# A decoder step on one core: the memory merge multiplied as rounded parts, and a third pair of split buffers from the output projection on

## The chip, the cores and the metric

The kernel runs on one core of one Trainium2 chip. The metric is device time in microseconds (us) of one execution, the median of several. The engines are TensorE (PE in the profile), VectorE (DVE), ScalarE (ACT), GpSimd (POOL) and SyncE (SP), which here only issues loads and stores.

## The reference, cut to what matters

One step of a hybrid decoder over 512 prompt tokens and 8 x 4 sample tokens (T = 544 columns in all), in float32. Three branches (latent attention, a state-space scan, attention into a memory) are projected, gated and summed; then come the output projection, a layer norm, a feed-forward part in two halves, and a second layer norm.

```python
def _merge_ffn(x, o_mla, o_ssm, o_mem, g_raw, b_gate, w_o_mla, w_o_ssm, w_o_mem, w_out,
               ln1_g, ln1_b, w_up, b_up, w_down, b_down, ln2_g, ln2_b):
    g = jax.nn.sigmoid((g_raw + b_gate).astype(F32)).astype(x.dtype)
    g_a, g_b, g_m = jnp.split(g, N_BRANCH, axis=-1)
    m = g_a * (o_mla @ w_o_mla) + g_b * (o_ssm @ w_o_ssm) + g_m * (o_mem @ w_o_mem)
    x1 = _layer_norm(ALPHA * x + m @ w_out, ln1_g, ln1_b)
    h = jnp.square(jax.nn.relu(x1 @ w_up + b_up))
    return _layer_norm(ALPHA * x1 + h @ w_down + b_down, ln2_g, ln2_b)
```

The change concerns the term `g_m * (o_mem @ w_o_mem)` with its gate projection (the memory merge), the product with `w_out` and the first layer norm.

## The kernel before

Activations lie with features on the 128 partitions and the 544 tokens in the free dimension, 8 chunks of 128 features for a width of 1024. Weights come as one stream of 128 x 1024 blocks (512 KB), loaded by SP into a ring of four slots; a block gives one output chunk of 128 features from 8 input chunks. There are two accumulators in PSUM, acc[0] and acc[1], each with two halves of 272 tokens.

A block is multiplied in one of two ways.
- As float32 (`project`, L1650 to L1665): 16 matmuls, which the profile shows as 32 instructions.
- As rounded parts (`project_parts`, L1706 to L1727, with `products`, L1700): weight and activation are each the sum of a rounded part and a remainder, both of type fp32r, and a product becomes three matmuls (rounded x rounded, rounded x remainder, remainder x rounded), 48 for a block. The activations' parts are made once; each weight block is split on its way: ACT copies it from the ring into a rounded buffer (L674), POOL subtracts that from the block into the remainder buffer (L498).

All order is written out by hand, with semaphores. `hi_ready` passes a block from ACT to POOL, `split_ready` from POOL to PE, and PE increments `split_begun` with the first matmul of a block. There are two pairs of split buffers, so that ACT may fill the pair of block i once block i-1 has begun (and block i-2 is therefore over).

The stages that the text speaks of, in order:
- Memory attention: PE reads cached values in (`cached_mem_values`), interleaved with the first merge. Its last piece increments `mem_used` to 16.
- Memory merge (phase merge_m, L2172 to L2181): for each of 8 output chunks j a float32 block with the gate weights on X (accumulator 0) and a float32 block with w_o_mem on the branch output BR (accumulator 1). ACT turns accumulator 0 into the gate (`read_gate`, L876). DVE multiplies it with accumulator 1 (L1584), adds it to the sum MG (L1588), rounds it (L1590, MG_H) and takes the remainder (L1592, MG_L, then `mg_ready`). Between the first two blocks PE turns the sample part of the memory attention, which DVE copies into BR (L1577).
- Output projection (out): 8 split blocks on MG_H, MG_L; `sums` on DVE adds accumulators to X and collects means and squares.
- First layer norm: `normalize` on DVE (L1050 to L1100), roots, gain and rounding on ACT (L653 to L663), half of the centring and of the remainders on POOL (L508, L512). Its normed chunks come one after the other, and `project_pair` multiplies each with the first two up blocks at once, so that both pairs of split buffers are in use until its end.
- Up and down projections in two halves (up0, down0, up1, down1), all as rounded parts; then the second layer norm and the stores.

## Time and profile before

| | us |
|---|---|
| median of 3 runs | 1771.91 |
| lowest, highest | 1770.88, 1776.06 |
| the profiled execution, its own time | 1772.24 |
| its span, first to last instruction | 1770.6 |
| TensorE busy in it | 1697.0 (96%) |
| mean granted TensorE clock | 0.984 of full |

The profile is of one execution. Its times count from the first instruction. A busy time is the union of an engine's instructions, a mean is of one instruction; matmuls overlap, so the distance from start to start says what one costs. "PE" rows are matmuls, "PEld" rows weight loads that run beside them. In square brackets at the end of a timeline row stands the idle time before it and what ended it.

### The profile page before, as it was taken

Reading aid. Unit: us, or ns where it says so; the run is one execution under the profiler, and the core shown is the slowest. Engines: PE = TensorE matmul, PEld = TensorE weight load, DVE = VectorE, ACT = ScalarE, POOL = GpSimd, SP = SyncE. Lnnn points to the kernel's source line nnn. Section 1 sums busy time; section 2 is a strip of 40 time slices with the busy share of each in tenths; the row PEclk is TensorE's granted clock in tenths of the full one; section 3 lists DMA queues with packets and bytes.
Section 4 is the critical chain, followed back from the end, with each engine's and each line's share of the span. In section 5 each row is a group of like instructions: output and inputs, shape, how many; then the busy total and the mean of one; then the engine's idle time right before and its main releaser. Section 6 shows DMA issues by size and latency. Waiting matters only on the chain.

```text
span 1770.6 us, 25324 instructions
## 1 busy us (share of the span) xinstructions
PE 1697.0 (96%) x10214; PEld 1417.9 (80%) x10214; DVE 741.8 (42%) x1296; ACT 380.9 (22%) x762; POOL 371.4 (21%) x330
## 2 busy tenths in 40 slices
PE   8999999999999999999999999999996999999995
PEld 6767777777877778777777777778895999999995
DVE  5657677674332111112122222311167771167345
ACT  2252432425212111111111110100124111111122
POOL 0041221403110000000333300100034343344332
PEclk9999999999999999999999999999998999999998
DMA  5324233252262222222777774422230322322221
GB/s 199 131 78 165 69 110 123 78 181 78 99 214 61 71 72 66 65 65 87 225 248 234 238 251 190 157 86 76 75 91 29 96 84 84 96 84 84 95 73 51
DMA packets 70406, 206.19 MB, mean 116 GB/s; under 512 B 10161, under 2 KB 26802, under 8 KB 65682
## 3 DMA queue, kind: packets, MB, share of 16 engines
q1 hardware_dynamic: 50384, 151.67, 26.6%
q10 hardware_dynamic: 13762, 31.93, 5.2%
q0 software_dynamic: 6144, 20.98, 3.9%
q8 instruction: 81, 1.33, 0.3%
q14 instruction: 35, 0.29, 0.1%
HBM read 189.68 MB, written 14.86 MB: 116 GB/s over the span
## 4 chain that ended last, share of the span: by engine, by line
PE 89%; DVE 5%; ACT 2%; DMA 2%; issue 1%; SPq 1%; POOL 0%; POOLq 0%; ACTq 0%; DVEq 0%
PE acc L1662 37%; PE acc L1702 24%; PE acc L1973 6%; PE acc L1939 3%; PE acc L1921 2%; PE acc L2076 1%; PE bank L1988 1%; PE bank L2007 1%; PE bank L1989 1%; DVE work L1169 1%; PE bank L2090 1%; PE bank L1958 1%; PE bank L1964 1%; PE bank L2161 1%; PE bank L1842 1%
## 5 line engine op out<-in xcount | busy, mean ns | idle before, releaser
L1662 PE MATMUL acc<-xt,ring 128*128 128x272 f32 x2496 | 599.5, 398 | 3.7 <-DMA ring<-in_stream 3.7
L1662 PEld LDWEIGHTS acc<-xt,ring 128*128 128x128 f32 x2496 | 473.5, 192 | 113.9 <-issue 18.7
L498 POOL TENSOR_TENSOR f_parts<-ring,f_parts 128x1024 fp32r<-128x1024 f32 x72 | 173.5, 2409 | 392.8 <-ACT f_parts L674 392.8
L1702 PE MATMUL acc<-x_parts,f_parts 128*128 128x272 f32 x1664 | 236.8, 292 | 16.8 <-DVE x_parts L1098 11.2
L1702 PEld LDWEIGHTS acc<-x_parts,f_parts 128*128 128x128 f32 x1664 | 221.3, 191 | 19.9 <-issue 13.2
L1702 PE MATMUL acc<-f_parts 128*128 128x272 f32 x1536 | 194.3, 289 | 0.0
L1702 PEld LDWEIGHTS acc<-f_parts 128*128 128x128 f32 x1536 | 193.6, 188 | 0.2
L476 POOL DMA_DIRECT2D work<-in_page_cols x128 | 68.8, 538 | 476.9 <-PE bank L2028 367.1
L674 ACT ACTIVATE f_parts<-ring 128x1024 fp32r<-128x1024 f32 x72 | 76.5, 1063 | 336.3 <-PE acc L1702 332.0
L1973 PE MATMUL acc<-branch,ring 128*128 128x272 f32 x512 | 120.0, 393 | 0.0
L1973 PEld LDWEIGHTS acc<-branch,ring 128*128 128x128 f32 x512 | 96.1, 190 | 18.7
L1625 DVE TENSOR_SCALAR f_parts<-attended 128x544 fp32r<-128x544 f32 x32 | 80.3, 2510 | 1.1
L1169 DVE SCALAR_TENSOR_TENSOR work<-work,vecs 128x600 f32<-128x600 f32 x72 | 70.3, 976 | 2.5
L1662 PE MATMUL acc<-attended,ring 128*128 128x272 f32 x256 | 60.4, 394 | 0.5 <-DVE attended L1540 0.5
L1662 PE MATMUL acc<-branch,ring 128*128 128x272 f32 x256 | 60.1, 393 | 0.6 <-DVE branch L1577 0.6
L1662 PEld LDWEIGHTS acc<-attended,ring 128*128 128x128 f32 x256 | 48.2, 190 | 11.4 <-issue 1.2
L1662 PEld LDWEIGHTS acc<-branch,ring 128*128 128x128 f32 x256 | 48.6, 190 | 10.7 <-DVE branch L1577 0.8
L446 POOL TENSOR_TENSOR work<-work 128x384 f32<-128x384 f32 x32 | 37.0, 1158 | 89.1 <-ACT work L766 89.1
L1609 DVE TENSOR_TENSOR xt<-xt,acc 128x544 f32<-128x544 f32 x11 | 7.9, 721 | 111.8 <-PE acc L1702 111.8
L876 ACT ACTIVATE work<-acc,vecs 128x544 f32<-128x544 f32 x16 | 11.4, 715 | 196.7 <-PE acc L1662 196.7
L1702 PE MATMUL acc<-mg_parts,f_parts 128*128 128x272 f32 x256 | 51.1, 297 | 2.3 <-DVE x_parts L1592 2.3
L1939 PE MATMUL acc<-work,ring 128*128 128x272 f32 x192 | 48.4, 412 | 2.8 <-ACT work L858 2.8
(338 smaller groups left out, 1819.7 us busy)
## 6 DMA issues: line engine op xcount, KB each, us to landing
ring<-in_stream SPq DMA_DIRECT2D x216, 512.0 KB, 3.6
work<-in_page_cols POOLq DMA_DIRECT2D x128, 160.0 KB, 3.3
attended<-in_ssm_state ACTq DMA_DIRECT2D x8, 1024.0 KB, 6.2
work<-cum_rows SPq DMA_DIRECT2D x32, 256.0 KB, 4.5
out_ssm_s<-attended ACTq DMA_DIRECT2D x8, 1024.0 KB, 5.6
work<-in_ckv_rows ACTq DMA_DIRECT2D x64, 128.0 KB, 3.7
work<-in_ckv_rows SPq DMA_DIRECT2D x64, 128.0 KB, 3.1
work<-in_memk_cols SPq DMA_DIRECT2D x8, 1024.0 KB, 6.8
```

Source lines behind the costliest of these rows:

```text
L446: pool.tensor_tensor(r, r, C_[:, P:SEQ], MUL).then_inc(sem["c_scaled"], 1)
L476: pool.dma_start(keys[kq][:, i * KEYS_W:(i + 1) * KEYS_W], page_cols[p]).then_inc(sem[f"keys_in_slot{kq}"], 16)
L498: pool.tensor_tensor(split[j][1], ring[:, s * BLOCK:(s + 1) * BLOCK], split[j][0].bitcast(F), SUB).then_inc(sem["split_ready"], 1)
L674: act.activation(split[j][0], ring[:, s * BLOCK:(s + 1) * BLOCK], ACT.Copy).then_inc(sem["hi_ready"], 1)
L1169: dve.scalar_tensor_tensor(out=c, in0=ext[j][:, i:i + CL], scalar=tap(i), in1=c, op0=MUL, op1=ADD).then_inc(sem[signal], 1)
L1625: dve.tensor_scalar(hi, q, 1.0, None, MUL).then_inc(sem["dve_step"], 1)
L1662: m = pe.matmul(acc[p][:, half, 0:width], w[:, k * P:(k + 1) * P], x(kk)[:, half * width:(half + 1) * width], start=kk == 0, stop=kk == n_ ...
L1702: m = pe.matmul(acc_half, w[:, k * P:(k + 1) * P], x[:, kk, of], start=kk == 0 and n == 0, stop=kk == last and n == 2)
L1842: m = pe.matmul(bank[hp % 2][j * HEAD_DIM:(j + 1) * HEAD_DIM, c * P:(c + 1) * P], xdt[:, c, h * HEAD_DIM:(h + 1) * HEAD_DIM], toks(decay[h ...
L1921: m = pe.matmul(acc[p][:, 0, 0:N_MEM], w[:, k * P:(k + 1) * P], mem[:, k, :], start=k == 0, stop=k == KC - 1)
L1939: m = pe.matmul(acc[p][:, half, 0:HT], w[:, c * 256 + off:c * 256 + off + P], cq[:, c, half * HT:(half + 1) * HT], start=c == 0, stop=c == 2)
L1973: m = pe.matmul(acc[1][:, half, 0:HT], w[:, k * P:(k + 1) * P], BR[:, kk, half * HT:(half + 1) * HT], start=kk == 0, stop=kk == 2 * KC - 1)
```

## The change

- Of the 16 blocks of the memory merge the last 14 are multiplied as rounded parts. `MERGE_SPLIT = 14`, and splitting starts 14 blocks earlier in the stream (`SPLIT_FROM`). For this X is rounded on ACT into X0_H with remainders on DVE (X0_L), and BR into M_H and M_L. M_L first holds the rounded copy, from which DVE takes the remainder; once the float32 block on BR is over, ACT rounds BR again, in place, into M_H.
- Splits of merge blocks alternate between the two pairs of buffers as before. From the output projection on there are three pairs in turn (`split_of`), and ACT may fill the pair of block i once block i-2 has begun.
- The first two output blocks are multiplied together (`project_last_chunk_last`): chunks 0 to 6 of the one, then of the other, then chunk 7 of both.
- The first block after `project_pair` is split before that has ended: ACT copies it behind the roots of the layer norm, POOL subtracts it between its second and third remainders.
- The marker `gate_a_ready` becomes a second count of `act_over`, `normed_even` and `normed_odd` are called `low_even` and `low_odd`, and the buffer `o_m` moves to the start of its region.

```diff
-SPLIT_FROM = blocks_before("out")
+MERGE_SPLIT = 2 * (KC - 1)
+SPLIT_FROM = blocks_before("out") - MERGE_SPLIT
...
+        M_LOW_AT = 22288
+        with ExitStack() as for_merge:
+            for_merge.enter_context(nc.sbuf_tensor("under_low", [P, (D_INNER // P + KC) * T + M_LOW_AT], F))
+            m_low = for_merge.enter_context(nc.sbuf_tensor("m_low", [P, KC * T], R))
...
+        X0_H, X0_L = (f_parts[:, X0_AT + i * KC * T:X0_AT + (i + 1) * KC * T].rearrange("p (c t) -> p c t", t=T)
+                for i in range(2))
+        M_H, M_L = chunks(x_parts, 2 * KC)[:, 0:KC, :], chunks(m_low, KC)
...
+        def split_of(i):
+
+            if i < MERGE_SPLIT:
+                return split[i % 2]
+            n = (i - MERGE_SPLIT) % 3
+            return split[n] if n < 2 else third_out if i <= MERGE_SPLIT + KC else third_up
...
             pool.wait_ge(sem["mem_used"], 2 * DEC_BATCH)
-            for i in range(N_SPLIT[0] + 2):
+            t.skip("rounded", 2 * KC)
+            for i in range(MERGE_SPLIT + N_SPLIT[0] + 2):
                 split_block(i)
...
                     pool.tensor_tensor(X_L[:, c, of], X[:, c, of], X_H[:, c, of].bitcast(F),
-                            SUB).then_inc(sem["normed_odd"], 1)
-            for i in range(N_SPLIT[0] + 2, sum(N_SPLIT)):
+                            SUB).then_inc(sem["low_odd"], 1)
+                    if h == 0 and c == 3:
+                        split_block(MERGE_SPLIT + N_SPLIT[0] + 2)
+            for i in range(MERGE_SPLIT + N_SPLIT[0] + 3, MERGE_SPLIT + sum(N_SPLIT)):
                 split_block(i)
...
-                if i == N_SPLIT[0] + 1:
-                    t.skip("split_begun")
-                else:
-                    act.wait_ge(sem["split_begun"], t.next("split_begun"))
+                s, (hi, _) = (SPLIT_FROM + i) % RING, split_of(i)
+                if i < MERGE_SPLIT + 2:
+                    act.wait_ge(sem["split_begun"], CREDIT["split_begun"] + i)
+                elif i != MERGE_SPLIT + N_SPLIT[0] + 2:
+                    act.wait_ge(sem["split_begun"], CREDIT["split_begun"] + i - 1)
...
-            for j in range(KC):
-                read_gate(2, j)
-
             act.wait_ge(sem["mem_used"], 2 * DEC_BATCH)
+            for c in range(KC):
+                act.activation(X0_H[:, c, :], X[:, c, :], ACT.Copy).then_inc(sem["rounded"], 1)
             for s in range(RING):
                 t.skip(f"weights_in_slot{s}", 16 * loaded_before(SPLIT_FROM, s))
+            split_block(0)
+            read_gate(2, 0)
+            act.wait_ge(sem["sample_read"], 2)
+            act.wait_ge(sem["stored"], t.next("stored", 16))
+            for c in range(KC):
+                act.activation(M_L[:, c, :], BR[:, c, :], ACT.Copy).then_inc(sem["rounded"], 1)
+            t.skip("rounded", 2 * KC)
+            split_block(1)
+            act.wait_ge(sem["acc1_ready"], t.value("acc1_ready"))
+            for c in range(KC):
+                act.wait_ge(sem["low_even"], t.next("low_even", KC + 1 if c == 0 else 1))
+                act.activation(M_H[:, c, :], BR[:, c, :], ACT.Copy).then_inc(sem["high_ready"], 1)
+            for j in range(1, KC):
+                read_gate(2, j)
+                split_block(2 * j)
+                if j < KC - 1:
+                    split_block(2 * j + 1)
...
-            for i in range(5):
-                split_block(i)
+            for i in range(1, 6):
+                split_block(MERGE_SPLIT + i)
...
-            split_block(9)
             std()
+            split_block(MERGE_SPLIT + 10)
             gain_bias("ln1g", "ln1b", [(c, of) for of in halves for c in range(KC)], True)
...
+            for c in range(KC):
+                dve.wait_ge(sem["rounded"], t.next("rounded"))
+                dve.tensor_tensor(X0_L[:, c, :], X[:, c, :], X0_H[:, c, :].bitcast(F), SUB).then_inc(sem["low_even"], 1)
             dve.wait_ge(sem["sample_out"], t.next("sample_out"))
...
+            for c in range(KC):
+                dve.wait_ge(sem["rounded"], t.next("rounded"))
+                dve.tensor_tensor(M_L[:, c, :], BR[:, c, :], M_L[:, c, :].bitcast(F), SUB).then_inc(sem["low_even"], 1)
...
+            def project_last_chunk_last(xh, xl):
+
+                pair = [split_of(splits.next() - 1) for _ in range(2)]
+                for p in range(2):
+                    pe.wait_ge(sem[f"acc{p}_free"], t.next(f"acc{p}_free"))
+                    pe.wait_ge(sem["split_ready"], t.next("split_ready"))
+                    for half, of in enumerate(halves):
+                        for k in range(KC - 1):
+                            if p == 0 and half == 0:
+                                pe.wait_ge(sem["mg_ready"], t.next("mg_ready"))
+                            first, m = products(acc[p][:, half, 0:HT], *pair[p], xh, xl, k, k, KC - 1, of)
+                            if (p, half, k) == (0, 0, 0):
+                                first.then_inc(sem["split_begun"], 1)
+                pe.wait_ge(sem["mg_ready"], t.next("mg_ready"))
+                for p in range(2):
+                    for half, of in enumerate(halves):
+                        first, m = products(acc[p][:, half, 0:HT], *pair[p], xh, xl, KC - 1, KC - 1, KC - 1, of)
+                        if (p, half) == (1, 0):
+                            first.then_inc(sem["split_begun"], 1)
+                    m.then_inc(sem[f"acc{p}_ready"], 1)
...
+            for j in range(1, KC):
+                project_parts(0, X0_H, X0_L, chunk_ready="low_even" if j == 1 else None)
+                project_parts(1, M_H, M_L, chunk_ready="high_ready" if j == 1 else None)
+            t.skip("low_even", KC)
...
-            for c in range(KC):
-                project_parts(c % 2, MG_H, MG_L, chunk_ready="mg_ready" if c == 0 else None,
-                              between=part_sums if c == KC - 1 else None)
+            project_last_chunk_last(MG_H, MG_L)
+            for c in range(2, KC):
+                project_parts(c % 2, MG_H, MG_L, between=part_sums if c == KC - 1 else None)
```

What stands in the instruction streams, at three places. First TensorE, from the first gate block of the memory merge on; xt is X, branch is BR, ring holds unsplit weights. Before:

```order
L1662 MATMUL acc<-xt,ring 128x272 x16
L2177 MATMUL acc<-cst,work 128x128 x2
L1662 MATMUL acc<-branch,ring 128x272 x16
L1662 MATMUL acc<-xt,ring 128x272 x16
L1662 MATMUL acc<-branch,ring 128x272 x16
```

Now, where f_parts also holds the split weights and X0_H, X0_L, and x_parts is M_H:

```order
L1711 MATMUL acc<-xt,ring 128x272 x16
L2246 MATMUL acc<-cst,work 128x128 x2
L1711 MATMUL acc<-branch,ring 128x272 x16
L1751 MATMUL acc<-f_parts 128x272 x48
L1751 MATMUL acc<-x_parts,f_parts 128x272
L1751 MATMUL acc<-m_low,f_parts 128x272
L1751 MATMUL acc<-x_parts,f_parts 128x272 x2
```

The first two blocks are unchanged; behind them a block is 48 matmuls instead of 16.

Second ScalarE, from the end of the memory attention to the first output splits. Before:

```order
L950 ACTIVATE work<-bank 128x512 x2
L876 ACTIVATE work<-acc,vecs 128x544 x8
L964 ACT_TABLE_LOAD
L964 ACTIVATE act_mark<-act_mark 1x1
L674 ACTIVATE f_parts<-ring 128x1024 x5
L648 ACTIVATE work<-xt 128x544 x3
```

Now, up to the second of the seven turns of the loop:

```order
L977 ACTIVATE work<-bank 128x512 x2
L985 ACTIVATE f_parts<-xt 128x544 x8
L701 ACTIVATE f_parts<-ring 128x1024
L903 ACTIVATE work<-acc,vecs 128x544
L993 ACTIVATE m_low<-branch 128x544 x8
L701 ACTIVATE f_parts<-ring 128x1024
L999 ACTIVATE x_parts<-branch 128x544 x8
L903 ACTIVATE work<-acc,vecs 128x544
L701 ACTIVATE f_parts<-ring 128x1024 x2
```

Between the eight gate reads (L876, now L903) there stand now 24 roundings and the copies of the weight splits.

Third GpSimd, from the memory attention to the up projection (L508 is centring, L512 a remainder of the layer norm). Before:

```order
L490 TENSOR_TENSOR work<-work,cst 128x256 x8
L498 TENSOR_TENSOR f_parts<-ring,f_parts 128x1024 x10
L508 TENSOR_TENSOR xt<-xt,work 128x272 x8
L512 TENSOR_TENSOR x_parts<-xt,x_parts 128x272 x8
L498 TENSOR_TENSOR f_parts<-ring,f_parts 128x1024 x62
```

Now:

```order
L514 TENSOR_TENSOR work<-work,cst 128x256 x8
L522 TENSOR_TENSOR f_parts<-ring,f_parts 128x1024 x24
L533 TENSOR_TENSOR xt<-xt,work 128x272 x8
L537 TENSOR_TENSOR x_parts<-xt,x_parts 128x272 x2
L522 TENSOR_TENSOR f_parts<-ring,f_parts 128x1024
L537 TENSOR_TENSOR x_parts<-xt,x_parts 128x272 x6
L522 TENSOR_TENSOR mg_parts<-ring,mg_parts 128x1024
```

There are 14 more weight remainders ahead of the layer norm, and one has moved in among its own remainders.

## Rows read from the trace of the kernel before

**Rows 1.** The page: busy times, and loads of weight blocks with time to landing
```profile
PE 1697.0 (96%) x10214; PEld 1417.9 (80%) x10214; DVE 741.8 (42%) x1296; ACT 380.9 (22%) x762; POOL 371.4 (21%) x330
...
ring<-in_stream SPq DMA_DIRECT2D x216, 512.0 KB, 3.6
```

**Rows 2.** Windows: stretch, its length, busy time by engine, granted clock, DMA
```profile
1177.66:1280.10 102.44, 102.44 (x449) 84.98 (x448) 18.33 (x28) 7.44 (x10) 2.35 (x1) 1.00 0.24 72
...
1282.90:1285.42 2.52, 0.23 (x3) 0.01 (x2) 2.43 (x2) 0.00 (x0) 1.40 (x1) 1.00 0.95 345
1285.42:1289.50 4.08, 4.08 (x20) 4.08 (x21) 0.00 (x0) 0.00 (x0) 0.00 (x0) 0.58 0.35 123
...
1368.00:1371.60 3.60, 0.09 (x1) 0.00 (x0) 3.53 (x3) 0.93 (x1) 2.48 (x1) 0.95 0.00 0
1371.60:1375.60 4.00, 3.96 (x21) 3.99 (x22) 3.90 (x5) 1.06 (x1) 2.11 (x1) 0.61 0.34 131
...
1379.60:1687.00 307.40, 307.40 (x2445) 307.40 (x2444) 153.93 (x139) 54.10 (x51) 122.33 (x51) 1.00 0.29 87
```

**Rows 3.** Waits of TensorE's matmuls from 1140 us on: total, times, longest
```profile
PE acc L1702 <- DVE x_parts L1098: 11.2, 3, 9.1
PE acc L1702 <- POOL f_parts L498: 3.5, 1, 3.5
PE acc L1702 <- DVE x_parts L1592: 2.3, 1, 2.3
```

**Rows 4.** Timeline of ScalarE: start, duration, line, operation, idle before
```profile
1169.46 0.71 ACT L876 ACTIVATE work<-acc,vecs 128x544 f32<-128x544 f32 x1 [23.30 <-PE acc L1662]
...
1280.70 1.06 ACT L674 ACTIVATE f_parts<-ring 128x1024 fp32r<-128x1024 f32 x1 [4.34 <-issue]
1290.81 1.06 ACT L674 ACTIVATE f_parts<-ring 128x1024 fp32r<-128x1024 f32 x1 [9.04 <-PE acc L1702]
...
1305.34 0.66 ACT L648 ACTIVATE work<-xt 128x544 f32<-128x544 f32 x1 [0.48 <-DVE xt L1029]
...
1372.29 1.06 ACT L674 ACTIVATE f_parts<-ring 128x1024 fp32r<-128x1024 f32 x1 [3.36 <-PE acc L1702]
1379.47 1.06 ACT L674 ACTIVATE f_parts<-ring 128x1024 fp32r<-128x1024 f32 x1 [6.12 <-PE acc L1702]
1385.51 1.06 ACT L674 ACTIVATE f_parts<-ring 128x1024 fp32r<-128x1024 f32 x1 [4.98 <-PE acc L1702]
```

**Rows 5.** Timeline of GpSimd
```profile
1281.91 2.40 POOL L498 TENSOR_TENSOR f_parts<-ring,f_parts 128x1024 fp32r<-128x1024 f32 x1 [3.04 <-ACT f_parts L674]
...
1338.69 2.35 POOL L498 TENSOR_TENSOR f_parts<-ring,f_parts 128x1024 fp32r<-128x1024 f32 x1 [7.12 <-ACT f_parts L674]
...
1351.36 0.76 POOL L512 TENSOR_TENSOR x_parts<-xt,x_parts 128x272 fp32r<-128x272 f32 x1 [2.46 <-ACT x_parts L663]
```

**Rows 6.** Timeline of VectorE
```profile
1161.95 0.42 DVE L1573 COPY work<-acc 128x256 f32<-128x256 f32 x1 [1.40 <-PE acc L2114]
1169.67 0.49 DVE L1577 COPY branch<-acc 128x128 f32<-128x128 f32 x2 [7.30 <-PE acc L2177]
...
1267.44 0.44 DVE L1590 TENSOR_SCALAR mg_parts<-work 128x544 fp32r<-128x544 f32 x1
1267.92 0.72 DVE L1592 SCALAR_TENSOR_TENSOR x_parts<-work,mg_parts 128x544 fp32r<-128x544 f32 x1
...
1282.11 2.49 DVE L1590 TENSOR_SCALAR mg_parts<-work 128x544 fp32r<-128x544 f32 x1
...
1338.92 0.43 DVE L1061 TENSOR_SCALAR work<-bank 128x272 f32<-128x272 f32 x1
1339.39 1.95 DVE L1064 SCALAR_TENSOR_TENSOR work<-work 128x272 f32<-128x272 f32 x1
...
1352.59 0.44 DVE L1080 TENSOR_TENSOR xt<-xt,work 128x272 f32<-128x272 f32 x1
...
1372.47 0.78 DVE L1619 TENSOR_SCALAR attended<-acc,vecs 128x544 f32<-128x544 f32 x1
```

More of the change, by code:

```diff
@@ L382, in program @@
         k.at = 0
+        o_m = k(N_MEM)
         m_prob = [k(N_MEM) for _ in range(NB)]
@@ L385, in program @@
         ms_prob, ms_prob_t = k(N_MEM), k(2 * P).rearrange("p (b n) -> p b n", b=2)
-        o_m = k(N_MEM)
         m_stats = [k(4) for _ in range(NB + 1)]
@@ L405, in program @@
         split = [[k(BLOCK) for _ in range(2)] for _ in range(2)]
+        THIRD_AT = 12576
+        third_out = [f_parts[:, THIRD_AT + i * BLOCK:THIRD_AT + (i + 1) * BLOCK] for i in range(2)]
+        third_up = [mg_parts[:, 4 * T + i * BLOCK:4 * T + (i + 1) * BLOCK] for i in range(2)]
+        assert after_heads + 2 * T <= THIRD_AT and THIRD_AT + 2 * BLOCK <= keys_at
+        def split_of(i):
[3 more added lines that the diff above has]
+            return split[n] if n < 2 else third_out if i <= MERGE_SPLIT + KC else third_up
         X_H, X_L = chunks(x_parts, 2 * KC)[:, 0:KC, :], chunks(x_parts, 2 * KC)[:, KC:2 * KC, :]
@@ L1643, in _ @@
             t = Counts(pe, {})
-            used = Count(None)
+            used, splits = Count(None), Count(None)
             def next_block():
@@ L1711, in project_parts @@
                 for b in range(n_blocks):
-                    j = (p * n_blocks + b) % 2
+                    wh, wl = split_of(splits.next() - 1)
                     pe.wait_ge(sem["split_ready"], t.next("split_ready"))
@@ L1718, in project_parts @@
                                 pe.wait_ge(sem[chunk_ready], t.next(chunk_ready))
-                            first, m = products(acc[p][:, half, 0:HT], *split[j], xh, xl, k, kk, n_blocks * KC - 1, of)
+                            first, m = products(acc[p][:, half, 0:HT], wh, wl, xh, xl, k, kk, n_blocks * KC - 1, of)
                             if half == 0 and k == 0:
@@ L1726, in project_parts @@
                 m.then_inc(sem[f"acc{p}_ready"], 1)
+            def project_last_chunk_last(xh, xl):
[17 more added lines that the diff above has]
+                    m.then_inc(sem[f"acc{p}_ready"], 1)
             def project_pair(xh, xl):
+                pair = [split_of(splits.next() - 1) for _ in range(2)]
                 for p in range(2):
```

56 lines of the change are left out of this document (28 added, 28 removed).

## The prediction, on record before the changed kernel had run

> **What bounds the kernel now.** I began with the busy times [rows 1]: TensorE is busy 96% of the span, no other engine over 42%. So only its work and its few waits count. The windows come next [rows 2]. From 1177.66 to 1280.10 us it multiplies the last 14 blocks of the memory merge as float32 without a break, at full granted clock (1.00): 102.44 / 14 = 7.32 us a block. Then its waits from there on [rows 3]: 2.3 us once on the last merged chunk (VectorE, L1592), 3.5 us once on a weight remainder (GpSimd, L498), 11.2 us on the normed chunks (9.1 of them the bulk of the first layer norm). The timelines of the three helpers say what stands ahead of each wait.
>
> A wait costs more than its length. After the 2.52 us in which matmuls were busy for 0.23, the next 4.08 us ran at a granted clock of 0.58; after the 3.60 us with 0.09, the next 4.00 ran at 0.61 [rows 2]. Of the two levels, 1.2 and 2.4 GHz, that is mostly the lower one. What it costs can be read from ScalarE, which starts each weight copy a fixed time after a block begins [rows 4]: from 1379.47 to 1385.51 is an undisturbed block of rounded parts, 6.04 us. The first output block took 1290.81 - 1280.70 = 10.11, that is 4.07 too long, and the first block behind the pair 1379.47 - 1372.29 = 7.18, 1.14 too long, behind a wait of 3.5.
>
> The Trainium skill has such a rule (TensorE: Matmul & The Clock Gate, section HAM oscillation): idle gaps drop the engine to half its clock, so that a stall is paid again in slow matmuls. The two windows agree, with 0.58 and 0.61.
>
> **Part 1, the 14 blocks.** Removed: 102.44 us. Added: 14 x 6.04 = 84.56. Gain 17.9 us, if the parts and splits are always there in time. That 6.04 holds for these operands rests on the stretch from 1379.60 to 1687.00, with clock 1.00 and matmuls busy throughout, which mixes blocks on x_parts and on f_parts [rows 2].
>
> What hides the new work, at the entry. `mem_used` is complete about 1161.9, when VectorE starts its copy [rows 6]. ScalarE then rounds X: 8 x 0.66 (the squaring of one 128x544 chunk [rows 4]) = 5.3, to 1167.3. VectorE's eight remainders keep that pace and end about 1168.1, since each is 0.72 and they overlap a little. Split 0: copy 1.06 to 1168.4, GpSimd 2.40 [rows 5] to 1170.9. The gate read at 1169.46 [rows 4] finds ScalarE free, and the sample copies at 1169.67 [rows 6] find VectorE free, so the second float32 block starts at 1170.22 as before. It covers the roundings of BR (8 x 0.66 from 1170.3, to 1175.6) and the remainders (VectorE, held until 1171 by split 0, then 8 x 0.72 as L1592 [rows 6], to 1177). Split block 0 begins at 1177.66, with all inputs there. Split 1 may start only then: copy from 1178.3, ready 1181.8, wanted at 1183.7. The rounding of BR in place follows, from 1179.4 to 1184.7; its chunk 7 is wanted at 1186.4. Then gate, copy and remainder for block 2: 0.71 + 1.06 + 2.40 and hand-overs give 1189.1, wanted at 1189.74. So the tightest place has 0.6 us to spare. Queued behind these on ScalarE is only the next split.
>
> In the loop, a gate block's end releases the gate read and at once the next-but-one split: 0.2 + 0.71 + 1.06 + 2.40 + 0.3 of hand-overs = 4.7 us, against a block of 6.04. The other split of a turn has no gate before it. VectorE's four merge steps per turn, 0.7 each, or 2.5 where GpSimd is in the way (L1590: 0.44 alone, 2.49 beside a split [rows 6]), have 12 us. Loads: a slot is asked for again once its block is split, some 20 us before the next split from it, and a load lands in 3.6 us [rows 1]. All this costs nothing while the 1.3 us of slack hold. With the cover gone at each of the seven gates, bounds are 0 and, from the worst delay that a row shows for a step (2.05, 2.49 - 0.44) less the slack, 7 x 0.75 = 5.2 us. I take 0.
>
> **Part 2, the entry of the output projection.** The last merged chunk is wanted now after the first seven of both blocks: 14/16 of 12.08 = 10.6 us after the merge ends. The chain of accumulator to `mg_ready` took until 1285.4, 5.3 us after 1280.1, and may take 7.5 if VectorE is held twice. So the 4.07 goes, clock loss included. New: accumulator 0 is complete only at 11.3, and VectorE's reading of it (0.2 + 0.78, as L1619 [rows 6]) ends 0.2 to 0.3 after the two blocks. Bounds for this wait 0 and 0.8. I take 0.3. Gain 3.8 us.
>
> **Part 3, the first layer norm.** Four terms.
> - The split at 1338.69 (2.35) [rows 5] leaves the tail: L1064 at 1339.39 took 1.95 beside it [rows 6], in a chain that all normed chunks wait for. L1080, of the same size and with two inputs too, takes 0.44 alone [rows 6]. Gain 1.5.
> - The split of the first block behind the pair is now put after the second remainder (1351.36 + 0.76 [rows 5]), so it runs from 1352.2 to 1354.6 of the old clock. VectorE's L1080 at 1352.59 [rows 6] wants to run just then. A step caught so at its start ends 0.3 after the split (L1590: 1284.60 against 1284.31), so 1354.9 instead of 1353.03: loss 1.9. Every later chunk hangs on it. Bounds 0 (if GpSimd comes behind) and 2.4.
> - The wait of 3.5 and the 1.14 of slow matmuls go, since the block is split already. Left is the read of accumulator 0 by VectorE, about 0.5. Gain 3.0 + 1.1 = 4.1.
> - GpSimd then has two remainders back to back (blocks 2 and 3 behind the norm), where it had a pause. VectorE's remainder of the hidden chunk falls between, and so its read of accumulator 1, at 1372.47 before [rows 6], comes after the second, about 1375.0 + 0.8; TensorE wants that accumulator at 1374.6. Loss 1.1; bounds 0 and 2.4.
>
> Net gain 1.5 - 1.9 + 4.1 - 1.1 = 2.6 us, bounds -1.3 and 5.6.
>
> On the second and fourth term the Trainium skill is plain (SBUF — State Buffer, section Who interferes with whom): a VectorE instruction with two SBUF inputs, or in a two-port mode, and a GpSimd instruction shut each other out for a whole instruction, and whoever starts first wins; with PSUM as a source it isn't held. The trace agrees on both sides: L1590 and L1064 were held, L1061 at 1338.92, which reads a bank, took 0.43 inside the same split. Without that rule the second term would be 0.3 and the norm's gain 4.2.
>
> **The rest.** Renamed semaphores and the moved `o_m` change no order. In the down stages a split may come one block sooner; nothing waits for splits there: one such wait in all [rows 3].
>
> **Sum.** 17.9 + 3.8 + 2.6 = 24.3 us. The profiled execution took 1772.24, 1.64 over its span of 1770.6, and 0.33 over the median of 1771.91. So 1770.6 - 24.3 = 1746.3 of span, 1747.9 of its own time, and 1747.6 as a median.
>
> **Rivals.**
> - The splits in the merge are late at each gate. For it: 0.6 us of slack at the first, 1.3 later, and VectorE's steps can hold GpSimd by 0.7. Against: the up stage has VectorE busy 153.93 of 307.40 us beside 51 splits without a wait [rows 2]. 7 x 1 us gives 1754.6.
> - The entry into the split blocks stalls. If the first split starts before VectorE's last remainder, the sample copies wait behind it for 2.4, and the clock may fall for 1.1 to 1.6: about 4 us, 1751.6. For it: the two come within 0.4 us of each other.
> - The layer norm gives nothing: held steps and the longer gap between chunks (part of it then at the lower clock) eat what the third pair frees. 1747.6 + 2.6 = 1750.2. For it: only few idle gaps are left between VectorE's and GpSimd's steps there, and a held step moves all behind it.
> - The other way: GpSimd is not in VectorE's way in the norm, and there is no new wait on accumulators: 1747.6 - 1.9 - 1.1 - 0.3 = 1744.3.
> - Slower than before: each turn of the merge gets the fate of the first output block, a wait of 2.5 with the clock behind it, 4.07 in all: 7 x 4.07 = 28.5, against a gain of 24.3, so about 1776. It decides once the chain from gate to remainder takes 8.5 us instead of 4.7, so if GpSimd's subtraction took 6.2 us instead of 2.40. Against: it reads and writes tiles of the same form as in the rows, where it took 2.35 and 2.40 [rows 5].
>
> **How the numbers follow.** Forecast 0.60; late splits 0.12; entry stall 0.10; nothing from the norm 0.10; the better one 0.05; slower 0.03. Time 1747.6. The range takes in the better case nearly and most of the three worse ones: 1743.5 to 1754.0; a seventh or so lies outside, mostly above. A measurement of this kernel tells 0.3%, 5.3 us, from no change, and every case but the last lies at least 17 us below: faster 0.96, same 0.01, slower 0.03.
>
> **What would show it.** The 14 blocks from about 1177.7 to 1262.2, each 6.04, at clock 1.00 and with no wait on L522 rows. The out stage begins with no wait on L1641 and no window at 0.6. L1107, the former L1064, at about 0.44 in both halves. One VectorE step of about 2.3 us in the first half of the norm, beside a GpSimd split. Behind the pair a wait under 1 us, then perhaps 1 on accumulator 1. The prediction is wrong if matmuls of the merge start more than 0.13 us apart at full clock, if ScalarE's rounding of a chunk takes over 0.8 us (the first gate's slack is then gone), or if the windows of the merge show a clock under 1.

## The result, and the profile after

| us | before | changed |
|---|---|---|
| median of the first comparison (4 runs each) | 1771.39 | 1743.33 |
| lowest, highest | 1768.57, 1776.06 | 1739.47, 1744.65 |
| profiled execution, its own time | 1772.24 | 1744.65 |
| its span | 1770.6 | 1743.0 |

The ratio is 0.9835 [0.9815, 0.9854]. The forecast was 1747.6 in a range of 1743.5 to 1754.0. So the direction was right, the gain was 28.1 us instead of 24.3, and the time fell 0.17 us below the range.

First the page of the changed kernel: busy times, and the loads of weight blocks. They answer to [rows 1].

```profile
PE 1674.6 (96%) x10438; PEld 1413.3 (81%) x10438; DVE 761.0 (44%) x1312; ACT 407.9 (23%) x800; POOL 405.7 (23%) x344
...
ring<-in_stream SPq DMA_DIRECT2D x216, 512.0 KB, 3.6
```

TensorE has 224 matmuls more and 22.4 us less of work. Loads land as fast as before.

Then the windows, which answer to [rows 2]: the 14 blocks of the merge, the first three blocks of the output projection with a stretch inside them, the stretch ahead of the pair's first matmul and the one behind it, and the two blocks behind the pair. "The pair" is the first two up blocks, which `project_pair` multiplies together while the normed chunks arrive.

```profile
1175.64:1259.60 83.96, 83.96 (x672) 83.96 (x671) 32.80 (x28) 25.09 (x31) 33.66 (x14) 1.00 0.30 95
1259.62:1278.99 19.37, 19.31 (x152) 18.97 (x151) 11.52 (x8) 4.25 (x4) 10.12 (x4) 1.00 0.35 107
1266.00:1270.00 4.00, 4.00 (x34) 4.00 (x33) 1.01 (x1) 0.00 (x0) 0.43 (x1) 1.00 0.58 192
1318.30:1321.80 3.50, 0.00 (x0) 0.00 (x1) 3.43 (x6) 1.92 (x4) 3.50 (x5) 0.50 0.00 0
1321.80:1325.80 4.00, 3.82 (x17) 3.52 (x18) 3.62 (x6) 2.14 (x5) 1.54 (x3) 0.59 0.00 0
1344.50:1357.50 13.00, 12.41 (x96) 12.19 (x97) 12.62 (x11) 2.52 (x3) 7.53 (x3) 1.00 0.31 93
```

The reader is to see the merge's blocks without a gap at full clock, and no stretch at 0.6 at the entry of the output projection any more. The window lies a little inside the blocks: their 672 matmuls (14 x 48) start at 1175.42, and the first one of the output projection at 1259.85, so the 14 blocks took 84.4 us, 6.03 each. The waits of TensorE from 1140 us on, to be held against [rows 3]:

```profile
PE acc L1751 <- DVE x_parts L1141: 11.4, 3, 7.6
PE acc L1751 <- POOL x_parts L537: 1.2, 5, 0.4
PE acc L1751 <- DVE attended L1668: 1.1, 2, 0.6
```

The waits on the merged chunk (2.3) and on the weight remainder (3.5) are gone, and 1.1 us on accumulators is new. The largest part of the wait for the normed chunks fell from 9.1 to 7.6.

ScalarE in the merge (start, duration, idle before) answers to [rows 4]:

```profile
1159.92 4.48 ACT L985 ACTIVATE f_parts<-xt 128x544 fp32r<-128x544 f32 x8 [15.80 <-PE acc L2185]
1164.31 1.05 ACT L701 ACTIVATE f_parts<-ring 128x1024 fp32r<-128x1024 f32 x1
...
1177.05 4.49 ACT L999 ACTIVATE x_parts<-branch 128x544 fp32r<-128x544 f32 x8
1181.86 0.71 ACT L903 ACTIVATE work<-acc,vecs 128x544 f32<-128x544 f32 x1 [0.31 <-PE acc L1751]
...
1193.94 0.72 ACT L903 ACTIVATE work<-acc,vecs 128x544 f32<-128x544 f32 x1 [4.85 <-PE acc L1751]
...
1205.97 0.72 ACT L903 ACTIVATE work<-acc,vecs 128x544 f32<-128x544 f32 x1 [4.85 <-PE acc L1751]
```

Eight roundings took 4.48 us, 0.56 a chunk, where 0.66 was reckoned. That is not because a rounding is shorter than the squaring that the 0.66 was read from: each lasts 0.64, but in a row they overlap, and the prediction took the length of one for the distance of two. So the first gate read at 1181.86 found ScalarE idle for 0.31, and the split behind it, the tightest place of the forecast, was ready at 1186.05 (GpSimd, 1183.66 + 2.39) and wanted at 1187.64: 1.6 us to spare where 0.6 was forecast. From 1193.94 to 1205.97 are two blocks, 12.03 us.

Now the layer norm and the two blocks behind it, TensorE first, then VectorE, then GpSimd ([rows 5, 6]):

```profile
1321.83 3.08 PE L1751 MATMUL acc<-x_parts,f_parts 128*128 128x272 f32 x12 [7.61 <-DVE x_parts L1141]
...
1331.08 1.04 PE L1751 MATMUL acc<-x_parts,f_parts 128*128 128x272 f32 x6 [3.65 <-DVE x_parts L1141]
...
1344.54 6.30 PE L1751 MATMUL acc<-x_parts,f_parts 128*128 128x272 f32 x48 [0.50 <-DVE attended L1668]
1351.40 6.30 PE L1751 MATMUL acc<-x_parts,mg_parts 128*128 128x272 f32 x48 [0.56 <-DVE attended L1668]
1357.54 7.72 PE L1751 MATMUL acc<-x_parts,f_parts 128*128 128x272 f32 x60
```
```profile
1313.82 0.44 DVE L1107 SCALAR_TENSOR_TENSOR work<-work 128x272 f32<-128x272 f32 x1
...
1326.81 2.15 DVE L1123 TENSOR_TENSOR xt<-xt,work 128x272 f32<-128x272 f32 x1
...
1347.84 2.80 DVE L1676 TENSOR_TENSOR f_parts<-attended,f_parts 128x544 fp32r<-128x544 f32 x1
```
```profile
1326.31 2.35 POOL L522 TENSOR_TENSOR f_parts<-ring,f_parts 128x1024 fp32r<-128x1024 f32 x1
...
1344.97 2.54 POOL L522 TENSOR_TENSOR mg_parts<-ring,mg_parts 128x1024 fp32r<-128x1024 f32 x1 [2.01 <-ACT mg_parts L701]
1347.59 2.48 POOL L522 TENSOR_TENSOR f_parts<-ring,f_parts 128x1024 fp32r<-128x1024 f32 x1
```

L1107 (L1064 before) is at 0.44. L1123 at 1326.81 was caught beside the split put among the remainders, and TensorE waited 3.65 in the pair where it had waited 1.94 (before):

```profile
1355.14 1.03 PE L1702 MATMUL acc<-x_parts,f_parts 128*128 128x272 f32 x6 [1.94 <-DVE x_parts L1098]
```

Behind the pair GpSimd has two splits back to back, and L1676 is held through the second.

Cut where the same matmul of the program starts (the pair's end: where its last one ends), the two profiled executions differ so:

| stage | before | changed | gain | forecast |
|---|---|---|---|---|
| start to the merge's first gate block | 1161.82 | 1159.79 | 2.03 | none |
| from there to the first output block | 118.30 | 100.06 | 18.24 | 17.9 |
| first three output blocks | 23.10 | 19.15 | 3.95 | 3.8 |
| to the pair's first matmul | 44.38 | 42.83 | 1.55 | 1.5 |
| the pair | 20.49 | 22.21 | -1.72 | -1.9 |
| pair's end to the third block behind it | 17.04 | 13.50 | 3.54 | 3.0 |
| the rest | 385.44 | 385.44 | 0.0 | 0 |

One shift is to be taken out. Where rounded parts follow float32, the first matmul is recorded 0.03 us behind the last float32 one and the next only 0.33 later, so a cut there falls 0.2 early. Before, that is the first output block; now it is inside the merge (1175.42). So 0.20 of the 3.95 belongs to the merge: 18.45 and 3.75. The kernel with the merge in float32, below, shows it: its three output blocks take 19.35.

The parts of the change brought 25.6 us where 24.3 were forecast. 2.0 us lie ahead of everything that was changed. The experiments ask two things: whether each part is worth what its row says, and what the 2.0 us are.

### The profile page after: what moved, and what is told of

Read it like the earlier page. It is cut to its first block, busy times and chain, and to the rows that moved or that the text cites. A ratio compares the mean times of both kernels' runs of the same rounds, so it can differ in the third digit from the quotient of the medians.

```text
span 1743.0 us, 25870 instructions
## 1 busy us (share of the span) xinstructions
PE 1674.6 (96%) x10438; PEld 1413.3 (81%) x10438; DVE 761.0 (44%) x1312; ACT 407.9 (23%) x800; POOL 405.7 (23%) x344
## 3 DMA queue, kind: packets, MB, share of 16 engines
q8 instruction: 83, 1.36, 0.3%
## 4 chain that ended last, share of the span: by engine, by line
PE 88%; DVE 6%; DMA 2%; ACT 2%; issue 1%; SPq 1%; POOLq 0%; POOL 0%; ACTq 0%; DVEq 0%
PE acc L1711 31%; PE acc L1751 29%; PE acc L2044 6%; PE acc L2010 3%; PE acc L1992 2%; PE acc L2147 1%; PE bank L2059 1%; DVE work L1212 1%; PE bank L2078 1%; PE bank L2060 1%; PE bank L2161 1%; PE bank L2029 1%; PE bank L2035 1%; PE bank L2232 1%; PE bank L1913 1%
## 5 line engine op out<-in xcount | busy, mean ns | idle before, releaser
L1711 PE MATMUL acc<-xt,ring 128*128 128x272 f32 x2272 | 545.8, 398 | 2.7 <-DMA ring<-in_stream 2.7
L1711 PEld LDWEIGHTS acc<-xt,ring 128*128 128x128 f32 x2272 | 429.9, 191 | 103.7 <-issue 17.7
L1751 PEld LDWEIGHTS acc<-x_parts,f_parts 128*128 128x128 f32 x1408 | 196.1, 191 | 15.8 <-issue 8.0
L2044 PE MATMUL acc<-branch,ring 128*128 128x272 f32 x512 | 120.0, 392 | 0.0
L2044 PEld LDWEIGHTS acc<-branch,ring 128*128 128x128 f32 x512 | 96.0, 190 | 18.8
L1751 PE MATMUL acc<-f_parts,mg_parts 128*128 128x272 f32 x528 | 68.8, 289 | 0.0
L1751 PEld LDWEIGHTS acc<-f_parts,mg_parts 128*128 128x128 f32 x528 | 67.3, 188 | 0.2
L522 POOL TENSOR_TENSOR mg_parts<-ring,mg_parts 128x1024 fp32r<-128x1024 f32 x21 | 50.5, 2403 | 71.4 <-ACT mg_parts L701 71.4
L1751 PE MATMUL acc<-x_parts,mg_parts 128*128 128x272 f32 x480 | 62.1, 289 | 0.6 <-DVE attended L1668 0.6
L1751 PEld LDWEIGHTS acc<-x_parts,mg_parts 128*128 128x128 f32 x480 | 61.0, 188 | 0.8 <-DVE attended L1668 0.8
```

The source lines that it names most:

```text
L522: pool.tensor_tensor(lo, ring[:, s * BLOCK:(s + 1) * BLOCK], hi.bitcast(F), SUB).then_inc(sem["split_ready"], 1)
L1711: m = pe.matmul(acc[p][:, half, 0:width], w[:, k * P:(k + 1) * P], x(kk)[:, half * width:(half + 1) * width], start=kk == 0, stop=kk == n_ ...
L1751: m = pe.matmul(acc_half, w[:, k * P:(k + 1) * P], x[:, kk, of], start=kk == 0 and n == 0, stop=kk == last and n == 2)
L2044: m = pe.matmul(acc[1][:, half, 0:HT], w[:, k * P:(k + 1) * P], BR[:, kk, half * HT:(half + 1) * HT], start=kk == 0, stop=kk == 2 * KC - 1)
```

## The experiments

Since the start of the merge scatters between executions, each kernel is also judged by the time from that start (first gate block) to the end of its span. That is 608.8 for the kernel before and 583.2 for the changed one.

**The merge in float32 again, the rest as changed.**

```diff
-MERGE_SPLIT = 2 * (KC - 1)
+MERGE_SPLIT = 0
...
-                project_parts(0, X0_H, X0_L, chunk_ready="low_even" if j == 1 else None)
-                project_parts(1, M_H, M_L, chunk_ready="high_ready" if j == 1 else None)
+                project(0, of_x)
+                project(1, lambda c: BR[:, c, :])
```

> The changed kernel with the memory merge back in float32 and all else kept (third pair of buffers, last chunk last, early split behind the pair). Theory A (the stages add up: merge 18.45 us, output entry 3.75, layer norm and what follows it 3.36, and the 2.0 us ahead of the merge are only the scatter of executions): the merge's 16 blocks take 118.3 us again, the output projection starts without a wait on the merged chunk, and the time is 7.1 us below the kernel before (0.4%), about 1764.3. Theory B (the 2.0 us ahead of the merge belong to the change, whichever part): the first gate block starts at about 1159.8 in this kernel too, and the time is 9.1 us below. Theory C (the gains overlap, since the splits of the float merge start late): the entry gains nothing, 3.4 us below.

1764.85 us, ratio 0.9953 [0.9935, 0.9972]. The merge takes 118.30, as before; the three output blocks 19.35. From the merge's start (1164.30, not 1159.8, so theory B falls) to the end 601.7: 7.1 better than before, 18.5 worse than changed. Its waits from 1140 us on:

```profile
PE acc L1728 <- DVE x_parts L1124: 11.4, 3, 7.6
PE acc L1728 <- DVE attended L1645: 1.1, 2, 0.6
```

So the parts in the merge are worth 18.5, and what the rest of the change brings (3.75 at the output's entry, 1.55 - 1.72 + 3.54 = 3.37 in the norm and behind it, 7.1 in all) doesn't hang on them.

**The merge in parts, the rest as before**: two pairs of buffers throughout, output blocks one after the other, the old places of the splits in the norm.

```diff
-            n = (i - MERGE_SPLIT) % 3
-            return split[n] if n < 2 else third_out if i <= MERGE_SPLIT + KC else third_up
+            return split[i % 2]
```

> Only the memory merge as rounded parts; two pairs of buffers, the output blocks one after the other, and the layer norm's splits as in the kernel before. Theory A: 18.4 us below the kernel before (1.04%), about 1753; 14 blocks in 84.2 us; the wait on the last merged chunk is back, and behind it the slow clock (about 4.1 us over an undisturbed block), and the wait of 3.5 us behind the pair is back. Theory B: 20.4 below. Rival to the entry's account: with a split of weights running while the last chunk is rounded, the wait is longer than before by up to one split (2.4 us), since GpSimd holds both the rounding and the remainder on VectorE.

1752.69 us, ratio 0.9891 [0.9858, 0.9924]; merge 100.06; from its start 588.8. That is 20.0 better than before, 1.5 more than the merge's 18.45. Here is the wait on the merged chunk again, as in [rows 3] and no longer, so the rival with a longer one falls; but the clock behind it did not fall as in [rows 2]. The matmul that waited, and a window on the 4 us behind it:

```profile
1268.84 0.39 PE L1746 MATMUL acc<-mg_parts,f_parts 128*128 128x272 f32 x1 [2.28 <-DVE x_parts L1636]
```
```profile
1267.80:1271.80 4.00, 2.96 (x23) 2.96 (x24) 0.95 (x2) 0.00 (x0) 0.00 (x0) 1.00 0.45 131
```

The block took 8.63 us (ScalarE's copies at 1264.07 and 1272.70) instead of 10.11. The same wait costs 2.6 at full clock and 4.1 with the fall. What the merge has to do with it is not shown: the fall came in both executions of the kernel before whose traces exist (10.10 and 10.11 for that block).

**Three pairs, but the output blocks one after the other.**

```diff
-            project_last_chunk_last(MG_H, MG_L)
-            for c in range(2, KC):
-                project_parts(c % 2, MG_H, MG_L, between=part_sums if c == KC - 1 else None)
+            for c in range(KC):
+                project_parts(c % 2, MG_H, MG_L, chunk_ready="mg_ready" if c == 0 else None,
+                              between=part_sums if c == KC - 1 else None)
```

> The changed kernel, but the first two output blocks one after the other, each through all eight chunks. Theory A: VectorE finished the last merged chunk 7.4 us after the merge's end in the changed kernel, held by two splits in a row. The first block wants that chunk 2.7 us after its start, so the wait is 4.7 us and 1.1 to 1.6 us of slow clock follow: 5.9 to 6.3 us slower than the changed kernel, more than the 4.07 that the kernel before lost here. Rival: the wait is as before, 2.3 us, and the loss 3.8 us.

1750.9 us, ratio 0.9879 [0.9848, 0.991]; from the merge's start 589.5, 6.3 worse than changed. The matmul that waited, and the 4 us behind it:

```profile
1268.66 0.60 PE L1751 MATMUL acc<-mg_parts,f_parts 128*128 128x272 f32 x1 [4.31 <-DVE x_parts L1641]
```
```profile
1268.70:1272.70 4.00, 4.00 (x18) 4.00 (x19) 0.00 (x0) 0.00 (x0) 0.00 (x0) 0.50 0.36 131
```

A block of 12.76 us, 6.7 too long. With three pairs ScalarE may copy two weight blocks in a row, GpSimd subtracts two in a row, and VectorE's last two merge steps are held by one each (2.50 and 2.74 here, 2.53 and 2.81 at 1261.63 and 1264.20 in the changed kernel). Only the new order of the output blocks hides that. So the order is worth 6.3 us here, not the 3.8 that it replaces, and the rival that had it at 3.8 falls.

**The changed kernel again**, to tell whether its 2.0 us ahead of the merge are its own.

> The changed kernel again, to see how far executions scatter. Theory A: the ratio to the kernel before is 0.9856 (25.6 us less: 18.45 + 3.75 + 3.36), and the first gate block of the merge starts anywhere between 1159 and 1163 us. Theory B: the ratio is 0.9844 or lower (27.6 us) and the first gate block starts at about 1159.8 every time.

1745.0 us, ratio 0.9851 [0.9824, 0.9878]; merge from 1159.71; from there 583.2; the same long waits.

**The split of the first block behind the pair only after all remainders of the norm.**

```diff
-                    if h == 0 and c == 3:
-                        split_block(MERGE_SPLIT + N_SPLIT[0] + 2)
-            for i in range(MERGE_SPLIT + N_SPLIT[0] + 3, MERGE_SPLIT + sum(N_SPLIT)):
+            for i in range(MERGE_SPLIT + N_SPLIT[0] + 2, MERGE_SPLIT + sum(N_SPLIT)):
                 split_block(i)
```

> The changed kernel with GpSimd's subtraction for the first block behind the pair moved behind all its remainders of the layer norm. Theory A (that subtraction holds VectorE's centring step for the whole of its time, and every later chunk hangs on it): the 2.15 us step becomes 0.44, the stretch from the pair's first matmul to its last falls from 22.2 us to 20.5, but the subtraction now ends about 1.4 us after the pair, so the block behind it waits 1.4 instead of 0.5: net 0.8 us less from the pair's start to the block behind it. Rival (the longer stretch comes from the third pair or from TensorE's clock, not from the lock): the stretch stays 22.2 and the net is a loss of 0.9.

One run, 1749.78, with its merge starting at 1166.02; from there 582.1, 1.1 better than changed.

```profile
1335.60 5.95 PE L1749 MATMUL acc<-x_parts,f_parts 128*128 128x272 f32 x30 [1.92 <-DVE x_parts L1139]
...
1349.96 6.28 PE L1749 MATMUL acc<-x_parts,f_parts 128*128 128x272 f32 x48 [1.41 <-POOL f_parts L522]
1356.53 6.30 PE L1749 MATMUL acc<-x_parts,mg_parts 128*128 128x272 f32 x48 [0.30 <-DVE attended L1666]
```

The 3.65 is 1.92 again and the pair takes 20.5: the held step is the split's doing, and costs the 1.7. The rival (the third pair of buffers, or the clock) falls. Instead the block behind waits 1.41 for the late split. In this place the early split was worth less than its price.

**No two subtractions in a row behind the norm**: from the third block behind the pair on, ScalarE's copy waits one block longer.

```diff
+                elif i > MERGE_SPLIT + N_SPLIT[0] + 3:
+                    act.wait_ge(sem["split_begun"], CREDIT["split_begun"] + i)
                 elif i != MERGE_SPLIT + N_SPLIT[0] + 2:
                     act.wait_ge(sem["split_begun"], CREDIT["split_begun"] + i - 1)
```

> The changed kernel, but from the third block behind the pair on ScalarE may split block i only once block i-1 has begun, as with two pairs, so that GpSimd has no two subtractions in a row there. Theory A (two in a row hold VectorE's remainder of the hidden chunk for 2.80 us and with it its read of accumulator 1): the step is 0.73 again, the wait of 0.56 us ahead of the second block goes, and the first two blocks behind the pair take 12.2 us together instead of 12.8. Rival: the 0.56 comes from VectorE's own load after the norm, and stays.

One run, 1740.26; from the merge's start (1156.25) 582.4, 0.8 better. VectorE behind the pair, where L1678 is L1676 of the changed kernel:

```profile
1341.72 2.52 DVE L1676 TENSOR_SCALAR f_parts<-attended 128x544 fp32r<-128x544 f32 x1
1344.28 0.73 DVE L1678 TENSOR_TENSOR f_parts<-attended,f_parts 128x544 fp32r<-128x544 f32 x1
```

One step held instead of two, the wait of 0.56 on accumulator 1 is gone, and the two blocks take 12.16 instead of 13.00. So that wait cost 0.84: its 0.56, and the rest in the distances of matmuls on both sides of it.

**A fourth pair of buffers for that block**, so that its split is done between the two halves of the last squares, ahead of the norm.

```diff
+            if i == MERGE_SPLIT + N_SPLIT[0] + 2:
+                return fourth
...
-            squares(out_sq, (7, halves[0]), (7, halves[1]))
+            squares(out_sq, (7, halves[0]))
+            split_block(MERGE_SPLIT + 10)
+            squares(out_sq, (7, halves[1]))
             std()
-            split_block(MERGE_SPLIT + 10)
```

> The changed kernel with a fourth pair of buffers for the first block behind the pair, in a part of the tile that is written only later; it is split while TensorE still multiplies the last output block, ScalarE copying between the two half squares of the last chunk. Theory A (lock): no VectorE step of the norm is held by a weight subtraction, the stretch from the pair's first matmul to its last is 20.5 us instead of 22.2, and the wait behind it stays 0.5: 1.7 us faster than the changed kernel, from 1743 to 1745 down to about 1742. Rival (clock or buffers): no change. The difference is near what timing can tell, so the stretches decide.

1743.12 us, ratio 0.9839 [0.9824, 0.9855]; from the merge's start 581.4, 1.8 better. The pair and its wait take 21.00 instead of 22.71, with 1.94 as the longest wait inside, and no wait for a split behind it.

**Both together.**

> Both of the last two: the fourth pair, and no two subtractions in a row behind the norm. Theory A: 1.7 + 0.6 = 2.3 us faster than the changed kernel, about 1741.5 to 1742.5, ratio to the kernel before 0.983 to 0.984. Rival: within 0.5 us of the changed kernel.

1741.91 us (1739.29 to 1745.89), ratio 0.9832 [0.9818, 0.9845]; from the merge's start 580.6. The two gains add up (2.6 = 1.8 + 0.8). By its trace it is the fastest of all; by time alone it can't be told from the changed one.

**That split between the halves of the norm**, three pairs, spaced as above (`c == 7` in place of `c == 3`).

> Three pairs as in the changed kernel. The split of the first block behind the pair moves from behind the third remainder of the first half to behind the last one of that half, and the split of the second block behind it starts one block later, so that GpSimd has no two in a row. If each held VectorE step costs its 1.9 us wherever it falls in the chain of normed chunks, this gains only behind the pair, 0.8 us as in the run with splits spaced (12.16 for two blocks in place of 13.0), and the pair takes 22.2 still. The rival: between the halves a step of the second half is held while TensorE still has finished chunks of the first half to work on, so that half or more of the 1.7 us comes back, as with the fourth pair (21.0 from the pair's first matmul to the next block in place of 22.7). Ratio 0.983 to 0.985 either way; the rows decide.

1745.16 us, ratio 0.9851 [0.9819, 0.9883]; from the merge's start 583.3. (In the changed kernel that split stands behind GpSimd's second remainder of the first half, not the third.) The two blocks behind the pair gained their 0.8 (12.18), but pair and wait took 23.59, longer than 22.71 and than either expectation. VectorE beside the split's new place (GpSimd, third row):

```profile
1331.92 2.46 DVE L1143 TENSOR_TENSOR x_parts<-xt,x_parts 128x272 fp32r<-128x272 f32 x1 [1.05 <-ACT x_parts L690]
1334.30 1.36 DVE L1129 TENSOR_TENSOR xt<-xt,work 128x272 f32<-128x272 f32 x2
1331.72 2.36 POOL L522 TENSOR_TENSOR f_parts<-ring,f_parts 128x1024 fp32r<-128x1024 f32 x1
```

The split fell on VectorE's first remainder of the second half, 2.46 where the others take 0.44, and the two steps behind it took 1.36 where they take 0.79. The whole stretch, first in this kernel, then in the changed one:

```profile
1320.10:1343.69 23.59, 18.65 (x97) 16.37 (x97) 17.19 (x30) 14.52 (x30) 9.18 (x10) 0.80 0.08 24
```
```profile
1321.83:1344.54 22.71, 17.05 (x97) 14.95 (x97) 16.28 (x30) 14.40 (x30) 9.04 (x10) 0.85 0.08 25
```

The granted clock was lower here, but it does not set the length of this stretch: with the fourth pair, and with both changes, it was 21.00 and 20.99 at 0.85 and 0.82.

```profile
1324.23:1345.23 21.00, 17.31 (x97) 14.96 (x97) 14.59 (x30) 14.40 (x30) 6.76 (x9) 0.85 0.00 1
1325.61:1346.60 20.99, 17.62 (x96) 15.58 (x97) 14.58 (x30) 14.40 (x30) 6.78 (x9) 0.82 0.00 1
```

What sets it is when the chunks come. In all of these TensorE waits 0.15 to 0.18 for the last one, which it starts 22.06 us behind the pair's first matmul here, 21.18 in the changed kernel and 19.48 with the fourth pair. So the first expectation is the nearer one: a held step costs wherever it falls in the chain, here 2.6 us.

**What the 2 us ahead of the merge are.** The last question went to the kernel before and the changed one again.

> The kernel before, again. In the nine traces so far the memory merge begins anywhere from 1156.25 to 1166.02 us, though the code ahead of it is the same. In windows of 100 us the shortfall of the granted clock up to 1156 us adds up to 6 to 16 us, and the start less that shortfall is 1147.7 to 1150.7 in all. Theory C: the same waits of 1 to 6 us are followed by a fall of the clock in some executions and by none in others, and that sets the start; so here too the start less the shortfall is 1147.5 to 1151, and the rest of the kernel behind the start takes 608.8 (as in the first trace, 1770.6 - 1161.8) within 1.5. Theory A1 (some waits are themselves longer in some executions, a DMA's) has the waits of TensorE up to 1156 us add up to several us more or less than in the first trace, and the difference of starts explained by them. Time 1766 to 1776.

> The changed kernel, a third time. Theory C: start of the merge less the shortfall of the clock 1147.5 to 1151; from that start to the end 583.2 within 1.5 (1743.0 - 1159.8). Then the change proper is 608.8 - 583.2 = 25.6 us in these traces, and what is above it in the measured 28.1 is the draw of the clock in the stretches that the change doesn't touch. Theory A1 as in the other run. Time 1738 to 1749.

1764.47 and 1746.0 us, one run each. Merge from 1153.89 and 1161.15, so this time the kernel before was 7 us ahead. From there to the end 608.8 and 583.2, to a tenth what the first traces gave. All thirteen traces, with the shortfall of the granted clock (1 less the clock, times the length, summed over windows of 100 us up to 1156 us; a window's clock has two digits, so each window may add an error of up to 0.5):

| kernel | merge starts | shortfall | difference | start to end |
|---|---|---|---|---|
| before | 1161.8 | 13 | 1148.8 | 608.8 |
| before again | 1153.9 | 6 | 1147.9 | 608.8 |
| changed | 1159.8 | 10 | 1149.8 | 583.2 |
| changed, again | 1159.7 | 12 | 1147.7 | 583.2 |
| changed, a third time | 1161.2 | 10 | 1151.2 | 583.2 |
| float32 merge | 1164.3 | 15 | 1149.3 | 601.7 |
| parts only | 1163.7 | 13 | 1150.7 | 588.8 |
| output blocks plain | 1161.5 | 12 | 1149.5 | 589.5 |
| split after the norm | 1166.0 | 16 | 1150.0 | 582.1 |
| splits spaced | 1156.3 | 6 | 1150.3 | 582.4 |
| split between halves | 1158.0 | 9 | 1149.0 | 583.3 |
| fourth pair | 1162.2 | 13 | 1149.2 | 581.4 |
| fourth and spaced | 1163.6 | 15 | 1148.6 | 580.6 |

The starts spread over 12.1 us, the difference over 3.5 (the band given was 1147.5 to 1151; one trace lies 0.2 over it). So most of the spread is the clock. One place shows how: a wait of TensorE for VectorE in the sample stage, the same code in both kernels. Before, the matmuls and two windows:

```profile
342.90 0.70 PE L1883 MATMUL bank<-rounded 96*128 96x512 f32 x2 [2.09 <-DVE branch L1346]
343.44 5.52 PE L1662 MATMUL acc<-xt,ring 128*128 128x272 f32 x16
```
```profile
340.00:345.00 5.00, 2.91 (x11) 2.04 (x10) 4.79 (x12) 2.00 (x3) 0.01 (x1) 0.89 0.12 46
345.00:350.00 5.00, 5.00 (x33) 3.87 (x33) 1.96 (x6) 0.72 (x2) 1.62 (x1) 0.77 0.00 0
```

And in the changed kernel:

```profile
343.80 0.71 PE L1954 MATMUL bank<-rounded 96*128 96x512 f32 x2 [2.10 <-DVE branch L1389]
344.35 3.83 PE L1711 MATMUL acc<-xt,ring 128*128 128x272 f32 x16
```
```profile
340.00:345.00 5.00, 2.90 (x13) 2.13 (x12) 4.79 (x10) 1.18 (x2) 0.55 (x1) 1.00 0.27 100
345.00:350.00 5.00, 5.00 (x43) 4.00 (x42) 3.57 (x10) 1.53 (x4) 1.64 (x1) 1.00 0.00 0
```

The wait is 2.09 and 2.10; behind it the same 16 matmuls take 5.52 in one execution and 3.83 in the other. The theory that the waits themselves differ explains little: of the kernel before and its repetition, whose merges start 7.9 us apart, the nine largest rows of waits up to 1156 us add up to 31.6 and 32.0 us. The largest difference among them that goes the right way is 0.9, on a load (3.7 and 2.8).

## Why the prediction was right in its parts and wrong in its sum

- **Part 1** (17.9): 18.45, with the 0.20 of the shift. A block of the merge took 6.015 us, not 6.04 (12.03 for two), 14 x 0.025 = 0.35 of the 0.55; the remaining 0.20 is that shift, since the 102.44 was cut where float32 goes over to parts. The stretch quoted for 6.04, which includes blocks on other operands, was right to half a per cent. The cover held everywhere: no wait on a split, no late gate. The rivals of late splits and of a stalled entry fell, and with them the slower one. The tightest place had 1.6 us to spare, not 0.6, since roundings in a row overlap.
- **Part 2** (3.8): 3.75, and the experiment with plain order shows the mechanism. The prediction allowed for a chain that ends 7.5 us behind the merge if VectorE is held twice, and so it came: it ended at 1267.01, 7.2 us behind. It did not say that the splits running ahead bring this about by themselves: in plain order the wait would have been 4.3, not 2.3. And 1.5 of its 4.07 is a fall of the clock that need not come, as the kernel with parts only showed.
- **Part 3** (2.6): 3.37. Held step gone 1.55 (1.5). Held step new -1.72 (-1.9), shown by the kernels that take the split out of there (1.92 and 1.94 instead of 3.65). Behind the pair 3.54 (3.0). Both terms of that were mis-sized. The wait on accumulator 1 is there but cost 0.84 instead of 1.1, by the kernel with splits spaced. And the wait and slow clock that went were worth 4.4 instead of 4.1: the 7.18 was read from ScalarE's copies, which start 0.38 us behind the start of an undisturbed block, but started 0.65 behind that of the block at the lower clock (1372.29, block from 1371.64), so this block took 7.45. The lower bound of -1.3 does not follow from the bounds of the terms, which give 1.5 - 2.4 + 4.1 - 2.4 = 0.8. The rival in which the norm gives nothing fell. So did the better one, whose two losses both came; that its 1744.3 lies nearer to the measured median than the forecast is luck.
- On the held steps the Trainium skill (SBUF — State Buffer, section Who interferes with whom) was right: a VectorE instruction with two SBUF inputs and a GpSimd instruction shut each other out, though here they work on different tiles. The traces agree: 2.15 at 1326.81 and 2.80 at 1347.84, where 0.44 and 0.73 are the durations alone; spaced splits gave back 0.8, the fourth pair 1.8.
- **The step that failed** is the last: "So 1770.6 - 24.3 = 1746.3 of span". It takes the stages that the change does not touch as they stood in one execution, and the range, 1743.5 to 1754.0, was drawn from the rivals alone, with no term for them. The difference of 4.3 us to the measured median is 1.3 from the three parts, 2.0 from the start of the merge in the profiled pair, and 1.0 from where the profiled executions lie against their medians (1744.65 against 1743.33; 1772.24 against 1771.91). The first is a matter of sizes. The second goes with the clock's draw, which moves the start over 12 us in thirteen traces (shortfall 13 in the kernel before, 10 in the changed one). The third has no traces behind it; the four executions of the changed kernel had mean clocks of 0.987, 0.987, 0.989 and 0.990, and the higher the clock the shorter the time, which fits the same cause but does not show it. All three went the same way, which is luck: without any one of them the time would have been inside the range. A hint of the draw was at hand: the three times of before ran over 5.2 us, and that spread went into the chances, not into the range.

That the median moved by 28.1 and the change itself by 25.6 is within what such draws do: the repetitions gave 1745.0 and 1746.0 for the changed kernel, against 1771.39 and 1772.52, 26.4 and 26.5 us.

## What to carry to other kernels

Read a change from an anchor: cut the traces at one instruction just ahead of it and just behind it. Here that gave the same 583.2 three times and 608.8 twice, while the times of whole executions ran over 5 to 12 us. Give the range a term for the unchanged stages as wide as the times of before. And when one more buffer lets a helper run ahead, look for the engine that it then shuts out twice in a row.

## What was not expected of the hardware

- After a wait of 2.1 to 2.3 us of TensorE the granted clock fell in some executions and not in others, by the same code: 5.52 against 3.83 us for 16 matmuls, 10.11 against 8.63 for a block. After 4.31 it was 0.50 for the next 4 us. What decides it was not found.
- ScalarE rounds 128x544 chunks, one behind the other, in 4.48 us for eight, 0.56 each, though a single one lasts 0.64: they overlap.
- With GpSimd subtracting twice in a row, one VectorE step was held through each, 2.53 and then 2.81, so that a chain of two short steps took 5.4 us.
